# Inputs stage of a hybrid encoder layer: z of a tile beside the latents of the tile before it, and another order of the first loads

## The reference

```
h   = rmsnorm(x, norm_mix_g)
p   = h @ w_in          # columns: 256 q-latent | 128 kv-latent | 32 rope key | 1792 z | 2048 gates
lat = rmsnorm(c_kv, kv_norm_g);  kpe = rope(k_pe, pos)
q   = rmsnorm([q_nope, rope(q_rope)] of rmsnorm(c_q) @ w_uq)        # 8 heads of 96
k,v = of lat_all @ w_ukv, k again rmsnorm'd per head                # lat_all: past rows and new ones
zm  = z + (prev(z) - z) * mu                                        # prev: the row before, in time
```

## Time and profile before

| | us |
|---|---|
| median of three runs (1686.13 to 1688.06) | 1687.55 |
| profiled execution: its own time | 1686.57 |
| profiled execution: its span | 1684.7 |
| first instruction of the stage after this one | 370.59 |
| PE busy in the span | 1518.1 |

### The profile page before, as it was taken

The page is one execution under the profiler, slowest core; times in us unless marked ns, Lnnn a source line. Parts: engine busy times, 40 slices in busy tenths (PEclk is TensorE's granted clock), DMA queues, the critical chain, the costliest instruction groups (busy, mean ns, idle before and its releaser), DMA issues. The chain is left out here.

```text
span 1684.7 us, 38787 instructions
## 1 busy us (share of the span) xinstructions
PE 1518.1 (90%) x16352; PEld 1076.7 (64%) x16352; DVE 865.1 (51%) x1874; ACT 445.5 (26%) x882; POOL 102.2 (6%) x102
## 2 busy tenths in 40 slices
PE   4999999969999999999996788878998699989895
PEld 2888888845666666666666456653554577766663
DVE  2444554555566767767677466654776223211111
ACT  2222222223223233233321233333444111111110
POOL 0000000000000000000000000000000122323321
PEclk9999999979999999999998799989999699999998
DMA  8332221544132132121112534416843699999982
GB/s 318 140 120 87 93 88 62 189 143 148 57 125 85 61 124 71 61 100 46 64 39 59 131 76 99 99 49 240 344 150 138 223 341 342 345 343 331 316 273 44
DMA packets 101326, 259.55 MB, mean 154 GB/s; under 512 B 34240, under 2 KB 53328, under 8 KB 91824
## 3 DMA queue, kind: packets, MB, share of 16 engines
q1 hardware_dynamic: 93424, 239.92, 41.9%
q0 software_dynamic: 7744, 17.33, 4.4%
HBM read 205.32 MB, written 60.56 MB: 158 GB/s over the span
## 5 line engine op out<-in xcount | busy, mean ns | idle before, releaser
L527 PEld LDWEIGHTS a_ps<-a_hT,a_wz 128*128 128x128 f32 x1792 | 202.6, 192 | 3.8 <-issue 3.8
L527 PE MATMUL a_ps<-a_hT,a_wz 128*128 128x128 f32 x1792 | 204.0, 275 | 0.0
L1890 PE MATMUL d_ps<-late,d_oT 128*128 128x512 f32 x256 | 115.4, 598 | 1.5 <-DVE d_oT L1659 0.8
L2061 DVE COPY f_xT<-f_turned 128x384 f32<-128x384 f32 x32 | 17.9, 558 | 163.1 <-PE f_turned L2028 163.1
L1890 PEld LDWEIGHTS d_ps<-late,d_oT 128*128 128x128 f32 x256 | 46.7, 190 | 51.6 <-issue 50.2
L1437 ACT ACTIVATE late<-c_score,c_top 128x1024 f32<-128x1024 f32 (+8 forms) x72 | 50.6, 703 | 103.9 <-DVEq L1415 97.9
L1101 PE MATMUL b_ps<-r_wg,r_hT 128*128 128x512 f32 x128 | 64.7, 639 | 11.8 <-POOL b_S L759 9.9
L821 DVE TENSOR_TENSOR b_M<-b_ps,r_causal 128x512 f32<-128x512 f32 x72 | 46.4, 686 | 54.7 <-PE b_ps L1162 54.2
L2255 DVE TENSOR_SCALAR f_y<-f_down,table 96x512 f32<-96x512 f32 x32 | 23.9, 747 | 97.9 <-PE f_down L2054 97.9
L2054 PE MATMUL f_down<-wd,f_midT 128*96 128x512 f32 x160 | 72.5, 596 | 1.8 <-DVE f_midT L2073 1.8
L2043 PEld LDWEIGHTS f_gated<-f_xT,wgu 128*64 128x64 f32 x1280 | 56.4, 142 | 22.7 <-issue 22.7
(11 more groups left out here) (355 smaller groups left out, 2860.7 us busy)
## 6 DMA issues: line engine op xcount, KB each, us to landing
wgu<-w_gate_up SPq DMA_DIRECT2D x20, 2048.0 KB
late<-w_gate_up SPq DMA_DIRECT2D x12, 2048.0 KB
wd<-w_down SPq DMA_DIRECT2D x20, 1024.0 KB
late<-w_down SPq DMA_DIRECT2D x12, 1024.0 KB
r_hT<-hT_d SPq DMA_DIRECT2D x18, 512.0 KB, 4.0
b_hT<-hT_d SPq DMA_DIRECT2D x18, 512.0 KB, 4.1
gate_d<-b_logits SPq DMA_DIRECT2D x32, 256.0 KB, 2.6
late<-gate_d SPq DMA_DIRECT2D x8, 1024.0 KB, 5.8
```

Of the source, the lines that this page charges most:

```text
L527: mm = pe.matmul(banks[Z_BANKS[n % 2]][:, j * P:(j + 1) * P], wz[:, i, (g + j) * P:(g + j + 1) * P], hT[t % 2][:, i, :], start=(i == 0), s ...
L1890: mm = pe.matmul(banks[2 + u][:], oT[t % 2][:, HB * branch(u) + k, :], wo[:, HB * branch(u) + k, half(u)], start=(k == 0), stop=(k == HB - 1))
```

## The change

PE makes z one tile earlier: z(0) before the loop, z(t+1) in iteration t, beside the latents and heads of tile t. spread_root and normed run one tile further ahead too. shifted(t) moves into iteration t. SP stores h and loads x one tile earlier in its order, while store_zm(t-1) and load_for_mixing keep their places. The first loads are x, ident, g_mix, xT and the first z weights; the small constants go behind all the weights. PE no longer waits for w_ukv before its first matmul, and some waits are put in for buffers that are now shared otherwise.

```diff
@@ SP @@
+            load_x(0)
             sp.dma_start(ident[:], io["ident"]).then_inc(first_in, 16)
+            sp.dma_start(g_mix[:], io["norm_mix_g"]).then_inc(first_in, 16)
+            load_xT(0)
+            load_wz(0)
             sp.dma_start(cn[:, QL:], io["past_lat"]).then_inc(past_in, 16)
             sp.dma_start(kpe[:], io["past_kpe"]).then_inc(past_in, 16)
-            load_x(0)
-            load_xT(0)
-            sp.dma_start(g_mix[:], io["norm_mix_g"]).then_inc(first_in, 16)
-            sp.dma_start(wkv[:], io["w_ukv"]).then_inc(first_in, 16)
+            sp.dma_start(wkv[:], io["w_ukv"]).then_inc(wkv_in, 16)
+            load_wz(1)
+            load_x(1)
+            load_xT(1)
+            load_wz(2)
+            sp.dma_start(w[:], io["w_mla"]).then_inc(w_in, 16)
+            load_wz(3)
             for dst, src in ((wq[:], io["w_uq"]), (trigs[:], io["trig"].rearrange("t p n -> p t n")),
...
-            store_h(0)
             load_x(2)
             load_xT(2)
+            load_x(3)
+            store_h(0)
             store_v(PAST_T)
             store_qk(PAST_T)
+            store_h(1)
+            load_xT(3)
             for t in range(NT):
                 store_latents(t)
-                if t + 1 < NT:
-                    store_h(t + 1)
-                if t + 3 < NT:
-                    load_x(t + 3)
-                    load_xT(t + 3)
+                if t + 2 < NT:
+                    store_h(t + 2)
+                if t + 4 < NT:
+                    load_x(t + 4)
+                    load_xT(t + 4)
                 if t >= 1:
                     store_zm(t - 1)
@@ DVE @@
+            dve.wait_ge(first_in, 32)
+            root_mean(0)
+            normed(0)
             dve.wait_ge(past_in, 32)
             dve.sem_inc(c_ready, 1)
-            dve.wait_ge(first_in, 48)
-            root_mean(0)
-            normed(0)
             root_mean(1)
+            normed(1)
...
             latent_squares(0)
+            root_mean(2)
             for t in range(NT):
                 latents(t)
-                if t + 1 < NT:
-                    normed(t + 1)
-                if t >= 1:
-                    shifted(t - 1)
                 if t + 2 < NT:
-                    root_mean(t + 2)
+                    normed(t + 2)
+                shifted(t)
+                if t + 3 < NT:
+                    root_mean(t + 3)
                 heads_normed(t)
                 if t + 1 < NT:
                     latent_squares(t + 1)
-            shifted(NT - 1)
@@ ACT @@
             square(0)
             root(0)
+            copy_z(0, 0)
+            copy_cT(PAST_T)
+            copy_z(0, 1)
             square(1)
             root(1)
-            copy_cT(PAST_T)
             copy_qkv(PAST_T)
+            copy_z(0, 2)
+            copy_z(0, 3)
             head_roots(PAST_T)
             copy_p1(0)
             latent_root(0)
+            square(2)
+            root(2)
             copy_turned(PAST_T)
...
@@ PE @@
             spread_root(0)
-            pe.wait_ge(h_ready, 1)
+            project_z(0, 0)
             turn_latents(PAST_T)
+            project_z(0, 1)
+            pe.wait_ge(wkv_in, 16)
             heads(PAST_T)
+            project_z(0, 2)
+            spread_root(1)
+            project_z(0, 3)
             pe.wait_ge(w_in, 16)
             project(0)
             turn_heads(PAST_T)
             for t in range(NT):
+                if t + 2 < NT:
+                    spread_root(t + 2)
                 if t + 1 < NT:
-                    spread_root(t + 1)
-                project_z(t, 0)
+                    project_z(t + 1, 0)
                 turn_latents(t)
-                project_z(t, 1)
+                if t + 1 < NT:
+                    project_z(t + 1, 1)
+                if t == 0:
+                    pe.wait_ge(consts_in, 16 * 8)
                 heads(t)
-                project_z(t, 2)
-                project_z(t, 3)
                 if t + 1 < NT:
+                    project_z(t + 1, 2)
+                    project_z(t + 1, 3)
                     project(t + 1)
                 turn_heads(t)
```

More of the change, by code:

```diff
@@ L173, in inputs_stage @@
         qkT = sb("qkT", [QK, 2 * H, P])
-        (w_in, first_in, past_in, consts_in, ones_set, dve_step,
+        (w_in, wkv_in, first_in, past_in, consts_in, ones_set, dve_step,
          x_squared, r_ms, r_root, r_ready, spread_done, h_ready, z_done, z_copied, zm_ready, row_kept,
@@ L177, in inputs_stage @@
          qk_ready, qkT_done, qkT_copied, lat_stored, v_stored, qk_stored, zm_stored, shift_stored) = (sem(n) for n in (
-             "w_in first_in past_in consts_in ones_set dve_step "
+             "w_in wkv_in first_in past_in consts_in ones_set dve_step "
              "x_squared r_ms r_root r_ready spread_done h_ready z_done z_copied zm_ready row_kept "
@@ L237, in load_for_mixing, with load_wz @@
                 sp.dma_start(early["wg"][0][:], io["w_gates"][:, :, 0:512]).then_inc(early["wg_in0"], 16)
+            def load_wz(n):
+                g, k = GROUPS[n]
+                sp.dma_start(wz[:, :, g * P:(g + k) * P], io["w_z"][:, :, g * P:(g + k) * P]).then_inc(wz_in[n], 16)
+            load_x(0)
             sp.dma_start(ident[:], io["ident"]).then_inc(first_in, 16)
+            sp.dma_start(g_mix[:], io["norm_mix_g"]).then_inc(first_in, 16)
+            load_xT(0)
+            load_wz(0)
             sp.dma_start(cn[:, QL:], io["past_lat"]).then_inc(past_in, 16)
             sp.dma_start(kpe[:], io["past_kpe"]).then_inc(past_in, 16)
-            load_x(0)
-            load_xT(0)
-            sp.dma_start(g_mix[:], io["norm_mix_g"]).then_inc(first_in, 16)
-            sp.dma_start(wkv[:], io["w_ukv"]).then_inc(first_in, 16)
+            sp.dma_start(wkv[:], io["w_ukv"]).then_inc(wkv_in, 16)
[5 more added lines that the diff above has]
+            load_wz(3)
             for dst, src in ((wq[:], io["w_uq"]), (trigs[:], io["trig"].rearrange("t p n -> p t n")),
-                             (mu[:], io["vecs"][:, 0:ZT]), (shift_in[:], io["shift0"]),
                              (g_head[:, 1, :], io["k_head_norm_g"].partition_broadcast(P)),
@@ L250, in _ @@
                              (g_lat[:, 0:QL], io["q_norm_g"].partition_broadcast(P)),
-                             (g_lat[:, QL:], io["kv_norm_g"].partition_broadcast(P))):
+                             (g_lat[:, QL:], io["kv_norm_g"].partition_broadcast(P)),
+                             (mu[:], io["vecs"][:, 0:ZT]), (shift_in[:], io["shift0"])):
                 sp.dma_start(dst, src).then_inc(consts_in, 16)
[L253 to L257, removed]
-            store_h(0)
             load_x(2)
             load_xT(2)
+            load_x(3)
+            store_h(0)
             store_v(PAST_T)
             store_qk(PAST_T)
+            store_h(1)
+            load_xT(3)
             for t in range(NT):
                 store_latents(t)
-                if t + 1 < NT:
-                    store_h(t + 1)
-                if t + 3 < NT:
-                    load_x(t + 3)
-                    load_xT(t + 3)
+                if t + 2 < NT:
[3 more added lines that the diff above has]
+                    load_xT(t + 4)
                 if t >= 1:
@@ L314, in normed @@
                     dve.wait_ge(z_done, NG_Z * (t - 1))
+                    dve.wait_ge(p1_done, t - 1)
                     dve.wait_ge(h_stored[b], 16 * (t // 2))
@@ L484, in _ @@
             latent_root(0)
+            square(2)
+            root(2)
             copy_turned(PAST_T)
             for t in range(NT):
-                copy_z(t, 0)
+                if t + 1 < NT:
+                    copy_z(t + 1, 0)
                 copy_cT(t)
[L489 to L492, removed]
+                if t + 3 < NT:
+                    square(t + 3)
+                    root(t + 3)
+                if t + 1 < NT:
+                    copy_z(t + 1, 1)
                 copy_qkv(t)
-                copy_z(t, 2)
+                if t + 1 < NT:
+                    copy_z(t + 1, 2)
                 head_roots(t)
-                copy_z(t, 3)
                 if t + 1 < NT:
+                    copy_z(t + 1, 3)
                     copy_p1(t + 1)
@@ L506, in spread_root @@
                 if t >= 1:
-                    pe.wait_ge(cT_copied, turn(t - 1))
+                    pe.wait_ge(h_ready, t)
+                    pe.wait_ge(cT_copied, max(t - 1, 1))
                 pe.matmul(banks[C_BANK][:, 0:P], ones[:], diag[:], start=True, stop=True).then_inc(spread_done, 1)
@@ L521, in project_z @@
                     pe.wait_ge(wz_in[n], 16)
+                if n == 0:
+                    pe.wait_ge(h_ready, t + 1)
                 if NG_Z * t + n >= 2:
@@ L536, in turn_latents @@
                 pe.wait_ge(c_ready, turn(t) + 1)
-                if 0 <= t < NT - 1:
-                    pe.wait_ge(h_ready, t + 2)
+                if t != PAST_T:
+                    pe.wait_ge(h_ready, min(t + 3, NT))
```

(8 more changed lines are left out.)

## The result

The changed kernel takes 1718.28 us (median of 4, 1715.93 to 1721.37) against 1686.84 (median of 4, 1685.12 to 1688.06): ratio 1.0184, 95% interval [1.0157, 1.0211], 31.4 us slower. The forecast was 1714.5, in a range of 1700 to 1723. The profiled execution took 1721.37, the slowest of the four; its span is 1719.5.

The account below looks back on a forecast made before the run. PE's work was taken to bound the stage between its ends. Head -6.6, steady tiles 0 and tail +34.0 summed to +27.4 us, so 1714.0 for the profiled execution, stated as 1714.5, range 1700 to 1723.

Parts of the forecast that it names:

- first z matmul: Head: PE starts z(0) at 12.3 us, when its first weights land, between 11.6 and 14.2.
- idle ahead of the loop: Head: PE idles 3.6 us before the loop, because spread_root(2) waits for root_mean(2) behind latent_squares(0).
- slow restart: Head: after the idle time PE's clock is likely slow again, costing between 0 and 3.0 us, taken as 2.0.
- period: Steady tiles: the same matmuls in another order still take 37.2 us a tile; 0 added, up to 5 us over all.
- zm(6) landed: Tail: this store, queued behind the next stage's loads, lands 27.9 us after tile 7's start, and shifted(7) waits for it.
- next stage: Tail's end: the following stage begins 83.0 us after tile 7's start, near 398 in the trace.
- head, tail: Both ends of the stage: the head gains 6.6 us (4 to 9), the tail costs 34.0 us (27 to 36).
- The constants were no bound: Head: constants loaded last let the past tile's heads_normed end near 46, which project(0)'s end at 48.1 covers by 2 us.
- The limit of 16.7 us: Steady tiles: a zm store landing up to 16.7 us after its tile's start costs PE nothing, qk being wanted at 35.4.
- rival 4: Steady tiles: zm landing at 19 instead of 15 costs each of six tiles 2.3 us, giving 1728; chance 0.09.
- rivals 2 and 3: Tail: zm(6) slips past the loads by +8.6 (1688 us, chance 0.09) or lands amid them at +20 (1706.5, chance 0.09).
- The 7 us that the tail would cost with the waits gone: Tail: without the zm waits it still costs 7 us, since z(8) no longer lies beside the last tile's chain.

Follow-up runs that it names:

- e5: e1 with square(2), root(2) and root_mean(2) ahead of tile 0's latents and x(2) loaded ahead of the constants; 1685.39 us, ratio 0.9977 to the kernel before.
- e1: Changed kernel with each zm stored in its own iteration, store_zm(t) in place of store_zm(t-1); 1687.76 us, ratio 1.0003 to the kernel before.
- e2: Changed kernel with only store_zm(6) moved, into iteration 6 ahead of the next stage's loads; 1697.69 us, ratio 1.0053 to the kernel before.
- e3: Changed kernel with load_for_mixing moved behind store_zm(6) in iteration 7, no store moved; 1696.81 us, ratio 1.0050 to the kernel before.
- e6: e1 with parts of z(7) and z(8), project(8), shifted(7), shifted(8) and load_for_mixing reordered in the last iterations; 1680.32 us, ratio 0.9960 to the kernel before.
- e8: Kernel before with only w, x(1), xT(1) and the first z weights loaded ahead of the eight constants; 1687.26 us, ratio 1.0006.
- e7: e1 with both the edits of e5 and those of e6; 1676.94 us, ratio 0.9943 to the kernel before.

## Why the prediction was right

| step | forecast | measured |
|---|---|---|
| first z matmul | 12.3 | 13.55 |
| project(0) ends | 48.1 | 49.2 |
| idle ahead of the loop | 3.6 | 3.3 |
| loop starts | 52.6 | 53.40 |
| slow restart | 2.0 | 1.7 (38.93 - 37.2) |
| period | 37.2 | 37.2 |
| zm(6) landed, from tile 7's start at 315.5 | +27.9 | +28.8 |
| shifted(8) starts | +54.9 | +55.9 |
| next stage | +83.0 | +83.8 |
| head, tail | -6.6, +34.0 | -6.1, +34.8 |

- **The head.** The mechanism was right. The first z weights came 1.25 us later than taken: from x at 4.5 to 13.5 their 2.69 MB came at about 300 GB/s, and I had taken the 401 of a later window over the 289 of an early one. The engines weren't slower by that much. In 4.5 to 13.55 they moved 3.33 MB, 368 GB/s, so over 0.6 MB of it belonged to loads behind these, which the sum had left out. The constants were no bound, as said: DVE's L407 at 41.31 followed normed(1) directly, with no wait for them. The gap came from the order of the roots, and e5 took it away together with the restart.
- **The steady tiles.** The limit of 16.7 us was right and a close one: in tile 3 zm landed at +16.9 and heads_normed ended 18.4 later, where 18.7 had been worked out. The reason given for staying below it was not right. The store was issued 3.3 us earlier, as said, but in tiles 1 to 4 it took 7.6 to 9.4 us, directly behind the loads of x and xT, where it had taken 3.5 to 6.5 before. It landed at +15.9 to +16.9 and not at the 15 taken. In tiles 5 and 6, which have no such loads, it took 4.5 and 4.7. So the wait of rival 4 was there in every tile, and that it cost only 0.4 us was partly luck: by the same sum, a landing 3 us later would have cost PE 2 to 3 us in each of tiles 1 to 4.
- **The tail.** The store landed right behind the load, w_gates at 341.2 and zm at 344.3, so rivals 2 and 3 fell. e1, e2 and e3 show the causes and their prices: 26.6 us from e1 to the changed kernel, of which 19.1 are the wait for zm(6), 5.0 the wait for zm(7) and 2.5 that zm(8) is stored last. That last part is in the kernel before too, inside the 8.0 us to the next stage. DVE's wait in tile 7 was named as some 20 us and was 26.56; PE's idling was named as 20 and was 16.00, with 2.68 of standstill ahead of it. The 7 us that the tail would cost with the waits gone came out as 372.7 - 314.5 - 49.0 = 9.2 in e1, but in part by luck: the chain up to the last qk store was 4.6 us longer than worked out, and the stretch behind it 2.5 shorter. e6 shows that the uncovered chain is what costs here, since matmuls laid under it were nearly free.
- **Small slips.** By the earlier trace rows PE's clock fell 2.9 us after PE stopped and not 3.1 (0.61 is 0.22 us of the window at full clock). The 1.0 us between the profiled execution and the median went into the forecast only by half.
- **The sum.** 27.4 us were forecast for the stage and 28.7 came. The other 2.7 us of the medians lie behind it. In the profiled execution the score matmuls came 30.4 later and the experts' first 31.1 (1356.0 against 1324.9), the end 34.8. The profiled execution was 3.1 above its median, so the 34.8 overstates the difference. I don't have a cause for the rest. From the stage's end to the span's end it was 1314.1 us before, 1320.2 changed and 1311.3 in e1, with the same code there, and the kernel before by itself spread over 1681.5 to 1691.4 in 21 runs.

On the order of transfers, the part of the Trainium skill's page (DMA: Bandwidth & Descriptors, Queues, rings and completion order) that counted here was the ring order. That completion need not be in order the trace shows too: the 64 KB of lat, issued behind w_gates at 328.21, landed at 339.8, 1.4 us ahead of it. For the 896 KB of zm it bought nothing.

## What to carry to other kernels

When a stage is moved one step ahead, move the store that frees its buffer as well, and look at what else stands in that queue in the iteration where the wait now falls: here 14 loads for the next stage, some 5 MB, made a wait of 26.6 us of one that was 6.2 in the tile before. A store that nobody in the stage waits for still counts if it is the last one before the barrier (2.5 us here). Work made ahead of time leaves the end without cover, so the last iterations need an order of their own (e6, 10.1 us earlier than e1), and the time at which a filler is needed matters as much as its size.

## What the runs showed of the hardware that was not expected

- SP's issue of a load of x takes 0.43 us in the steady tiles. In the head, with several MB outstanding, single issues took 5.00 (x(1) at 6.63 in the changed kernel), 6.42 and 6.77 us (e8), and what stood behind them in SP's list was issued later by that. What holds an issue up wasn't tested.
- While the loads for the next stage ran, PE stood still inside project(8) without a semaphore to wait for: 2.68 us in the changed kernel (first row of its tail above), 1.28 in e1, 1.33 in e2, 2.16 in e3, 0.99 in e5, at the same place each time, behind its first matmul. It didn't occur in e6 and e7, where project(8) comes some 17 us earlier. What it waits for wasn't settled. In all five the instruction queue (q8 in the DMA view) moved one packet of 0.02 MB some 2 to 3 us ahead of the restart, and in e6 and e7 none while project(8) ran, which would fit a late fetch of instructions; no run tests it.
- In the kernel before, the granted clock reads 1.00 up to 32 us, although the 416-column matmuls from 28.48 on are at first twice as far apart (0.70) as later (0.35). After the 3.3 us gap of the changed kernel it reads 0.53 in 53.4 to 55.4, and the durations agree.
